# Turning the gate units of the second block with VectorE's block turn and ScalarE's copies

## The chip, the cores and the metric

The kernel runs on one core of a Trainium2 chip. The metric is the device time of one execution in microseconds. The kernel before takes 2195.05 us (median of 3 runs, 2194.01 to 2198.27).

## The reference, cut to what matters

Two blocks of a network run one after the other on 256 tokens of width 2048, everything in float32. The first is a gated linear attention with a convolution branch and a feed-forward part. The second, where the change is, makes eight projections of its input, runs two attentions (16 heads of a dilated one, 16 heads of a neighbourhood one), multiplies their outputs by silu of the two gate projections, multiplies that by `w_out` and ends in a layer norm:

```python
def second_block(x, w_in, w_out, t5_bias, na_rpb, ln_gain, ln_bias):
    ...
        h = jnp.einsum('bsd,de->bse', x, w_in[layer])
        qa, ka, va, ga, qb, kb, vb, gb = jnp.split(h, splits, axis=-1)
        ya = _dilated_attention(heads(qa, N_HEADS_A), heads(ka, N_HEADS_A), heads(va, N_HEADS_A), t5_bias)
        yb = _neighbourhood_attention(heads(qb, N_HEADS_B), heads(kb, N_HEADS_B), heads(vb, N_HEADS_B), na_rpb[layer])
        ya = merge(ya) * jax.nn.silu(ga.astype(jnp.float32))
        yb = merge(yb) * jax.nn.silu(gb.astype(jnp.float32))
        y = jnp.concatenate([ya, yb], axis=-1).astype(x.dtype)
        out = jnp.einsum('bse,ed->bsd', y, w_out[layer])
        x = _layer_norm(DEEPNORM_ALPHA * x + out, ln_gain[layer], ln_bias[layer])
```

## The kernel before, in words

**Units and steps.** All large products are cut into 96 units, the list `UNITS`: a unit is one 256 x 512 piece of a product, over 2048 rows of a weight. A unit has four steps, one for each 512 x 512 piece of the weight, so there are 384 steps, numbered s. Unit u has the steps 4u to 4u+3. The end of the list is: the units q2, k2, v2 of four head groups (steps 304 to 351), the gate units y0 to y3 (352 to 367), and the output units out0 to out3 (368 to 383).

**One step.** A float32 value is held as a sum of two numbers that TensorE multiplies fast (`hi` and `lo`). For each step SyncE loads 1 MB of weight into one of three `raw` buffers, ScalarE copies it to `whi` (`split`, L715), VectorE subtracts to get `wlo` (L981), and TensorE runs 24 matmuls (L1438 to L1440: 4 pieces of the contraction, 2 halves of the tokens, 3 products of hi and lo). In their program ScalarE and VectorE split for step s+2 while they are at step s; the split of step s+2 may begin when TensorE is through with step s-1, since the three buffers are used in turn. TensorE's `products(s)` waits for `s_lo`, which VectorE's split raises.

**Jobs.** The function `jobs(s)` lists what else each engine does at step s. Each engine walks through the steps in order and does its share of each job in the order in which its own function (`pool`, `scalar`, `vector`, `tensor`) is written. There is no scheduler: what stands first in the program of an engine runs first. The table `LATER` gives the jobs that follow a unit.

**The two ways to turn a unit.** The left operand of a product has to lie with the contraction on the partitions, so results have to be turned. The q, k and y units are turned by TensorE: `turn` (L1448) transposes eight 128 x 128 pieces into two of the four `side` banks of PSUM. The q2 and k2 units are turned in two parts: `block_turn` (L1203), one VectorE instruction that turns the 32 x 32 blocks in place into a buffer, and `carry` (L744), 16 ScalarE copies of 32 partitions x 256 elements that bring each block to its partitions, four in each of the jobs block, carry1, carry2, carry3.

**The gate units.** `post` of unit yj, at step 4u+3, applies silu on ScalarE (L793) and writes a `tmp` buffer. Two steps later the job `turn_y` follows, at steps 357, 361, 365 and 369 for y0 to y3: TensorE turns, VectorE multiplies YT (the attention's output, already turned) by the bank, in two halves (`times_gate`, L1169), ScalarE copies the product to `setA_hi` (L918), VectorE subtracts to `setA_lo` (L1360). In steps 357 and 361, which also have an attention job, `gate_turns(s)` puts the collection of the attention's values (`one_half`, L816 and L817, and `add_halves`, L1159) and `times_gate` ahead of the split. The output unit out0 needs in its step 368+c the product of gate unit yc, by the semaphore `s_yl` (`ready`, asked by TensorE in `products`).

**The attention.** Its last jobs are at steps 352 to 361: `att` 24 to 33. The values of the last pair of heads come at step 361.

Of the kernel before, what the change touches and what calls it, by code (L numbers as in the profile page):

```python
# [27 lines left out]
         "k2": ("block", "carry1", "carry2", "carry3"), "y": ("none", "turn_y")}  # L28
# [4 lines left out]
def jobs(s):  # L33
# [65 lines left out]
    for u in range(max(0, s // 4 - 2), s // 4 + 1):  # L99
        kind, j = UNITS[u]  # L100
        later = LATER.get(kind, ())
        if kind == "down" and j >= 12:
            later = ("flip", "flip_split")
        n = s - 4 * u - 4 if u > 0 else s - 7
        if 0 <= n < len(later):
            out.append((later[n], u))
# [4 lines left out]


def gate_turns(s):

    return any(job == "turn_y" for job, a in jobs(s))
# [74 lines left out]
def two_block_program(nc, T, C, out):  # L190
# [8 lines left out]
    with ctx:  # L199
# [24 lines left out]
        A_raw = at("setA_raw", "A", 16 * KB, [128, 16, 256])  # L224
        B_raw = at("setB_raw", "B", 16 * KB, [128, 16, 256])
# [141 lines left out]
        s_vh, s_yv, s_yh, s_yl = sem("s_vh"), sem("s_yv"), sem("s_yh"), sem("s_yl")  # L367
# [66 lines left out]
        def ready(u, kk):  # L434
# [17 lines left out]
            if kind == "out" and j == 0:  # L452
                return s_yl, part + 1
            return None

        def blocks(u):

            kind, j = UNITS[u]
            if kind in ("q2", "k2"):
                blk, turned = (qTb, qTr) if kind == "q2" else (kTb, kTr)  # L460
                return blk[j % 2][:, :, :, :, :], turned[j % 2][:, :, :], 1.0

# [242 lines left out]
        def scalar(e):  # L705
# [116 lines left out]
            for s in range(NS):  # L822
                for job, a in jobs(s):
                    if job == "att" and a % 2 and gate_turns(s):
                        one_half((a - 3) // 2)
# [7 lines left out]
                for job, a in jobs(s):  # L833
# [76 lines left out]
                    elif job == "turn_y":  # L910
                        j = UNITS[a][1]
                        e.wait_ge(*set_free(a))
                        e.wait_ge(s_xf, 2)
                        e.wait_ge(*full("values", 11 if j < 2 else 15))
                        for b in range(2):
                            k = 4 * j + 2 * b
                            e.wait_ge(*seen("turn", a, b))
                            e.activation(A_hi[:, k:k + 2, :], YT[:, k:k + 2, :], ACT.Copy).then_inc(s_yh, 1)  # L918
# [15 lines left out]
                    elif job == "att":  # L934
                        if a % 2 and a >= 3 and not gate_turns(s):
                            one_half((a - 3) // 2)
# [36 lines left out]
        def vector(e):  # L973
# [188 lines left out]
            def times_gate(u):  # L1162
                j = UNITS[u][1]
                e.wait_ge(*seen("values", 4 * j + 3))
                for b in range(2):
                    n = SN["turn", u, b]
                    v = YT[:, 4 * j + 2 * b:4 * j + 2 * b + 2, :]
                    e.wait_ge(*full("turn", u, b))
                    e.tensor_tensor(v, two(side[n % 4][:, :]), v, ALU.mult).then_inc(s_read[n % 4], 1)  # L1169

# [24 lines left out]
            def block_turn(u):  # L1195
# [5 lines left out]
                elif kind in ("q2", "k2"):  # L1201
                    e.wait_ge(s_xf, 2)
                e.transpose(blk.rearrange("p k t r n -> p t k (r n)"),  # L1203
# [25 lines left out]
            for s in range(NS):  # L1229
# [10 lines left out]
                for job, a in jobs(s):  # L1240
                    if job == "att" and a % 2 and gate_turns(s):
                        add_halves((a - 3) // 2)
                for job, a in jobs(s):
                    if job == "turn_y" and a < UI["y", 2]:
                        times_gate(a)
# [13 lines left out]
                for job, a in jobs(s):  # L1259
# [93 lines left out]
                    elif job == "turn_y":  # L1353
                        j = UNITS[a][1]
                        if j >= 2:
                            times_gate(a)
                        for b in range(2):
                            k = 4 * j + 2 * b
                            e.wait_ge(s_yh, 2 * j + b + 1)
                            e.tensor_tensor(A_lo[:, k:k + 2, :], YT[:, k:k + 2, :], asf(A_hi[:, k:k + 2, :]),  # L1360
# [292 lines left out]
```

## Time and profile before

| what | value |
|---|---|
| median of 3 runs | 2195.05 us |
| the execution that was profiled | 2196.3 us |
| its span, first to last instruction | 2193.6 us |
| granted TensorE clock, mean | 0.998 |
| TensorE busy | 2180.3 us, 99% of the span |
| VectorE busy | 1526.8 us, 70% |
| ScalarE busy | 1045.8 us, 48% |
| GpSimd busy | 228.4 us, 10% |
| chain that ended last | TensorE 91%, VectorE 5%, ScalarE 2% |

The profiled execution is 2.7 us longer than its span and 1.25 us above the median. A busy TensorE is not TensorE at its peak, because matmuls overlap: one of 128 x 512 is shown with 390 ns, but the next starts 227 ns after it.

### The profile page before, as it was taken

What the parts mean: (1) busy time and instruction counts of PE and PEld (TensorE: products, weight loads), DVE (VectorE), ACT (ScalarE), POOL (GpSimd) and SP (SyncE); (2) the same over time, 40 slices, a digit from 0 to 9 for tenths busy, and PEclk for the clock granted to TensorE, in tenths of its full rate; (3) what the DMA queues carried; (4) which work ended last, traced back from release to release, by engine and by line L of the source; (5) the groups of instructions that cost most, each with busy time, mean ns of one, the idle gap of its engine ahead of it and who ended that gap; (6) DMA issues with size and microseconds to landing.
All of it is one profiled execution on the core that took longest, in us unless ns stands there. A gap on an engine that the chain in (4) does not pass through costs nothing.

```text
span 2193.6 us, 24281 instructions
## 1 busy us (share of the span) xinstructions
PE 2180.3 (99%) x9962; PEld 1807.0 (82%) x9962; DVE 1526.8 (70%) x1613; ACT 1045.8 (48%) x1046; POOL 228.4 (10%) x253
## 2 busy tenths in 40 slices
PE   9999999999999999999999999999999999999998
PEld 8888888888888888888888888888888888888886
DVE  5577648646667747888855864864788778887755
ACT  7455554333333433444433433433444667767543
POOL 1023010000000000000100000000100122253201
PEclk9999999999999999999999999999999999999999
DMA  9555465777878776655555556566556756656663
GB/s 322 191 174 173 154 185 191 227 221 222 246 222 241 217 214 202 226 196 189 195 197 187 200 196 195 176 211 192 192 175 225 253 185 196 195 170 195 221 230 115
DMA packets 217102, 444.88 MB, mean 203 GB/s; under 512 B 9316, under 2 KB 10484, under 8 KB 216096
## 3 DMA queue, kind: packets, MB, share of 16 engines
q1 hardware_dynamic: 206976, 411.07, 56.6%
q0 software_dynamic: 9728, 32.18, 6.1%
q8 instruction: 78, 1.28, 0.2%
q14 instruction: 32, 0.26, 0.0%
q10 hardware_dynamic: 288, 0.10, 0.0%
HBM read 427.08 MB, written 12.06 MB: 200 GB/s over the span
## 4 chain that ended last, share of the span: by engine, by line
PE 91%; DVE 5%; ACT 2%; issue 1%; DMA 1%; POOL 0%; POOLq 0%; DVEq 0%; ACTq 0%
PE acc L1438 29%; PE acc L1439 29%; PE acc L1440 29%; DVE setB_raw L1192 1%; DVE wlo L981 1%; ACT whi L715 1%; PE side L1462 1%; DMA raw<-in_w_in 1%; PE side L1510 0%; PE side L1524 0%; PE side L1496 0%; DVE mx L1406 0%; ACT qTr L744 0%; DVE Sm L1402 0%; DVE PTl L1151 0%
## 5 line engine op out<-in xcount | busy, mean ns | idle before, releaser
L981 DVE TENSOR_TENSOR wlo<-raw,whi 128x2048 fp32r<-128x2048 f32 x380 | 892.9, 2352 | 512.0 <-ACT whi L715 510.7
L715 ACT ACTIVATE whi<-raw 128x2048 fp32r<-128x2048 f32 x380 | 726.8, 1914 | 668.6 <-PE acc L1440 641.2
L1438 PE MATMUL acc<-whi,setA_lo 128*128 128x512 f32 x1792 | 699.1, 390 | 0.1
L1440 PE MATMUL acc<-whi,setA_hi 128*128 128x512 f32 x1792 | 697.3, 389 | 0.0
L1439 PE MATMUL acc<-wlo,setA_hi 128*128 128x512 f32 x1792 | 697.3, 389 | 0.0
L1438 PE MATMUL acc<-whi,setB_lo 128*128 128x512 f32 x1280 | 501.2, 392 | 2.1 <-DVE wlo L981 1.1
L1439 PE MATMUL acc<-wlo,setB_hi 128*128 128x512 f32 x1280 | 498.6, 390 | 0.0
L1440 PE MATMUL acc<-whi,setB_hi 128*128 128x512 f32 x1280 | 498.1, 389 | 0.0
L1438 PEld LDWEIGHTS acc<-whi,setA_lo 128*128 128x128 f32 x1792 | 336.4, 188 | 71.2 <-DVE wlo L981 0.8
L1440 PEld LDWEIGHTS acc<-whi,setA_hi 128*128 128x128 f32 x1792 | 336.3, 188 | 70.3
L1439 PEld LDWEIGHTS acc<-wlo,setA_hi 128*128 128x128 f32 x1792 | 336.4, 188 | 68.7
L1438 PEld LDWEIGHTS acc<-whi,setB_lo 128*128 128x128 f32 x1280 | 240.3, 188 | 55.5 <-DVE setB_lo L1376 2.1
L1440 PEld LDWEIGHTS acc<-whi,setB_hi 128*128 128x128 f32 x1280 | 240.3, 188 | 50.5
L1439 PEld LDWEIGHTS acc<-wlo,setB_hi 128*128 128x128 f32 x1280 | 240.3, 188 | 48.6
L1192 DVE STREAM_TRANSPOSE setA_raw<-tmp 32x256 f32<-32x256 f32 x320 | 139.4, 436 | 9.4
L666 POOL TENSOR_TENSOR tmp<-tmp 128x1024 f32<-128x1024 f32 x16 | 30.4, 1897 | 733.4 <-DVE tmp L1109 733.4
L929 ACT ACTIVATE setA_hi<-setA_raw 128x1024 fp32r<-128x1024 f32 x20 | 21.3, 1063 | 96.2 <-DVE setA_raw L1192 96.2
L609 POOL TENSOR_TENSOR bia<-bia,msk 128x512 f32<-128x512 f32 x32 | 52.6, 1643 | 81.9 <-DMA bia<-t_scratch 44.9
L1192 DVE STREAM_TRANSPOSE setB_raw<-X 32x256 f32<-32x256 f32 x128 | 55.9, 436 | 3.8
L1192 DVE STREAM_TRANSPOSE setB_raw<-tmp 32x256 f32<-32x256 f32 x128 | 55.8, 436 | 3.8
L947 ACT ACTIVATE Sm<-Sm,nmx 128x256 f32<-128x256 f32 x64 | 32.1, 502 | 51.0 <-DVE nmx L1409 51.0
L646 POOL TENSOR_TENSOR DD<-cum 128x2048 f32<-128x2048 f32 x8 | 36.4, 4553 | 145.6 <-DVE cum L1293 91.2
(210 smaller groups left out, 1088.6 us busy)
## 6 DMA issues: line engine op xcount, KB each, us to landing
raw<-in_w_in SPq DMA_DIRECT2D x188, 1024.0 KB, 5.3
raw<-in_w_ffn_up SPq DMA_DIRECT2D x64, 1024.0 KB, 5.2
raw<-in_w_ffn_down SPq DMA_DIRECT2D x64, 1024.0 KB, 5.1
raw<-in_w_gla_out SPq DMA_DIRECT2D x16, 1024.0 KB, 5.1
raw<-in_w_conv_out SPq DMA_DIRECT2D x16, 1024.0 KB, 5.1
raw<-in_w_o SPq DMA_DIRECT2D x16, 1024.0 KB, 5.1
raw<-in_w_out SPq DMA_DIRECT2D x16, 1024.0 KB, 5.1
t_scratch<-t5v POOLq DMA_DIRECT2D x8, 512.0 KB, 7.2
```

The source lines that it names most:

```text
L609: e.tensor_tensor(bia[b][:, :, :], bia[b][:, :, :], msk[h // 16][:, :, :], ALU.add).then_inc(s_mb, 1)
L646: e.tensor_tensor(dv, cv, ref, ALU.subtract).then_inc(s_xd, 1)
L666: e.tensor_tensor(tm, tm, tm, ALU.mult).then_inc(s_pq, 1)
L715: e.activation(whi[r][:, :, :], raw[r][:, :, :], ACT.Copy).then_inc(s_hi, 1)
L929: e.activation(hi[:, k:k + 4, :], turned[:, k:k + 4, :], ACT.Copy).then_inc(s_fh, 1)
L947: e.activation(Sm[b][:, t, :], Sm[b][:, t, :], ACT.Exp, bias=nmx[b][:, t:t + 1], accum_out=den[b][:, t:t + 1]).then_inc(s_ex, 1)
L981: e.tensor_tensor(wlo[r][:, :, :], raw[r][:, :, :], asf(whi[r][:, :, :]), ALU.subtract).then_inc(s_lo, 1)
L1192: e.transpose(dst[32 * r:32 * r + 32, :, :, q, :], src[32 * q:32 * q + 32, :, :, r, :]).then_inc(s_fl, 1)
L1438: e.matmul(o, xl, whi[r][:, k, :], start=kk == 0, stop=False)
L1439: e.matmul(o, xh, wlo[r][:, k, :], start=False, stop=False)
L1440: f = e.matmul(o, xh, whi[r][:, k, :], start=False, stop=kk == 15)
L1462: f = e.matmul(bank[:, 128 * h:128 * h + 128], row[:, 0:128], row[:, 128:256], start=dd == 0, stop=dd == 1)
```

## The change

The gate units now take the second way of turning. TensorE's turns of the y units (32 transposes, four groups of eight) are gone, and with them their use of the `side` banks. For each gate unit there are three jobs instead: `block01` (VectorE's block turn of the unit's `tmp` into `A_blk`, then eight of ScalarE's carrying copies into `A_raw`), in the next step `carry23` (the other eight copies), and in the step behind that `gate_y` (VectorE multiplies YT by `A_raw`, ScalarE copies the whole 128 x 1024 to `setA_hi`, VectorE subtracts to `setA_lo`). The buffers lie in region A, which the attention uses until its end, and the jobs stand at steps 362, 363, 364 for y0, 364, 365, 366 for y1, 366, 367, 368 for y2 and 368, 369, 370 for y3. `gate_y` stands ahead of the split in the programs of both engines. `gate_turns` is gone, so the attention jobs of steps 357 and 361 stand behind the split as in all other steps. A new semaphore `s_yg` joins the multiplication to the copy.

```diff
-         "k2": ("block", "carry1", "carry2", "carry3"), "y": ("none", "turn_y")}
+         "k2": ("block", "carry1", "carry2", "carry3"), "y": ()}
...
-    for u in range(max(0, s // 4 - 2), s // 4 + 1):
+    for u in range(max(0, s // 4 - 3), s // 4 + 1):
...
+        if kind == "y":
+            later = ("none",) * (6, 4, 2, 0)[j] + ("block01", "carry23", "gate_y")
...
-def gate_turns(s):
-
-    return any(job == "turn_y" for job, a in jobs(s))
...
+        A_blk = at("setA_blk", "A", 0, [128, 16, 2, 4, 32])
...
-                return s_yl, part + 1
+                return s_yl, kk // 4 + 1
...
+            if kind == "y":
+                return A_blk[:, 4 * j:4 * j + 4, :, :, :], A_raw[:, 4 * j:4 * j + 4, :], 1.0
...
                 for job, a in jobs(s):
-                    if job == "att" and a % 2 and gate_turns(s):
-                        one_half((a - 3) // 2)
+                    if job == "gate_y":
+                        k = 4 * UNITS[a][1]
+                        e.wait_ge(s_yg, UNITS[a][1] + 1)
+                        e.activation(A_hi[:, k:k + 4, :], YT[:, k:k + 4, :], ACT.Copy).then_inc(s_yh, 1)
                 if s < 2:
                     fine(s + 2)
...
-                    elif job == "turn_y":
-                        j = UNITS[a][1]
-                        e.wait_ge(*set_free(a))
-                        e.wait_ge(s_xf, 2)
-                        e.wait_ge(*full("values", 11 if j < 2 else 15))
-                        for b in range(2):
-                            k = 4 * j + 2 * b
-                            e.wait_ge(*seen("turn", a, b))
-                            e.activation(A_hi[:, k:k + 2, :], YT[:, k:k + 2, :], ACT.Copy).then_inc(s_yh, 1)
...
-            def times_gate(u):
...
+                if kind == "y":
+                    e.wait_ge(*set_free(u))
+                    e.wait_ge(s_xf, 2)
+                    e.wait_ge(*full("values", 11 if j < 2 else 15))
                 e.transpose(blk.rearrange("p k t r n -> p t k (r n)"),
                             tmp_of(u)[:, :, :].rearrange("p t (k n) -> p t k n", k=4)).then_inc(s_bt, 1)
...
                 for job, a in jobs(s):
-                    if job == "att" and a % 2 and gate_turns(s):
-                        add_halves((a - 3) // 2)
-                for job, a in jobs(s):
-                    if job == "turn_y" and a < UI["y", 2]:
-                        times_gate(a)
+                    if job == "gate_y":
+                        j = UNITS[a][1]
+                        v = YT[:, 4 * j:4 * j + 4, :]
+                        e.wait_ge(*seen("values", 4 * j + 3))
+                        e.wait_ge(s_bm, 16 * BN[a] + 16)
+                        e.tensor_tensor(v, A_raw[:, 4 * j:4 * j + 4, :], v, ALU.mult).then_inc(s_yg, 1)
+                        e.wait_ge(s_yh, j + 1)
+                        e.tensor_tensor(A_lo[:, 4 * j:4 * j + 4, :], v, asf(A_hi[:, 4 * j:4 * j + 4, :]),
+                                        ALU.subtract).then_inc(s_yl, 1)
```

ScalarE's row before, from the split of step 368 to that of step 372 (L715 is a split, L793 silu of y3, L918 the copy of a gated product):

```order
L715 ACTIVATE whi_54<-raw_51 128x2048
L715 ACTIVATE whi_52<-raw_49 128x2048
L793 ACTIVATE tmp_65<-acc,rstd_150 128x512 x2
L715 ACTIVATE whi_53<-raw_50 128x2048
L715 ACTIVATE whi_54<-raw_51 128x2048
L918 ACTIVATE setA_hi<-YT 128x512 x2
L715 ACTIVATE whi_52<-raw_49 128x2048
```

The same stretch of ScalarE now (L744 are eight carrying copies, of y2 in the first two rows of it and of y3 in the last two; L827 is the copy of the gated product, of y2 and then of y3):

```order
L715 ACTIVATE whi_54<-raw_51 128x2048
L744 ACTIVATE setA_raw<-setA_blk 32x2x4x32 x8
L715 ACTIVATE whi_52<-raw_49 128x2048
L744 ACTIVATE setA_raw<-setA_blk 32x2x4x32 x8
L793 ACTIVATE tmp_66<-acc,rstd_151 128x512 x2
L827 ACTIVATE setA_hi<-YT 128x1024
L715 ACTIVATE whi_53<-raw_50 128x2048
L744 ACTIVATE setA_raw<-setA_blk 32x2x4x32 x8
L715 ACTIVATE whi_54<-raw_51 128x2048
L744 ACTIVATE setA_raw<-setA_blk 32x2x4x32 x8
L827 ACTIVATE setA_hi<-YT 128x1024
L715 ACTIVATE whi_52<-raw_49 128x2048
```

Between the same five splits stand 32 carrying copies that were not there, and one gated product's copy more.

VectorE's row before, from the split of step 368 to that of step 372 (L981 is a split, L1169 the two multiplications by the turned gate y3, L1360 its two subtractions):

```order
L981 TENSOR_TENSOR wlo_57<-raw_51,whi_54 128x2048
L981 TENSOR_TENSOR wlo_55<-raw_49,whi_52 128x2048
L981 TENSOR_TENSOR wlo_56<-raw_50,whi_53 128x2048
L981 TENSOR_TENSOR wlo_57<-raw_51,whi_54 128x2048
L1169 TENSOR_TENSOR YT<-side,YT 128x512 x2
L1360 TENSOR_TENSOR setA_lo<-YT,setA_hi 128x512 x2
L981 TENSOR_TENSOR wlo_55<-raw_49,whi_52 128x2048
```

The same stretch of VectorE now (L974 is the split, L1191 the block turn of y3, L1234 the multiplication and L1236 the subtraction, of y2 and then of y3):

```order
L974 TENSOR_TENSOR wlo_57<-raw_51,whi_54 128x2048
L974 TENSOR_TENSOR wlo_55<-raw_49,whi_52 128x2048
L1191 STREAM_TRANSPOSE setA_blk<-tmp_66 128x2x4x128
L1234 TENSOR_TENSOR YT<-setA_raw,YT 128x1024
L1236 TENSOR_TENSOR setA_lo<-YT,setA_hi 128x1024
L974 TENSOR_TENSOR wlo_56<-raw_50,whi_53 128x2048
L974 TENSOR_TENSOR wlo_57<-raw_51,whi_54 128x2048
L1234 TENSOR_TENSOR YT<-setA_raw,YT 128x1024
L1236 TENSOR_TENSOR setA_lo<-YT,setA_hi 128x1024
L974 TENSOR_TENSOR wlo_55<-raw_49,whi_52 128x2048
```

The block turn of y3 and the gate of y2 stand ahead of the split of step 370, and the gate of y3 stands behind the split of step 371, ahead of that of step 372.

## Rows read from the trace of the kernel before

**Rows 1.** The page's first part: busy time of each engine.
```profile
PE 2180.3 (99%) x9962; PEld 1807.0 (82%) x9962; DVE 1526.8 (70%) x1613; ACT 1045.8 (48%) x1046; POOL 228.4 (10%) x253
```

**Rows 2.** All waits of TensorE: us in total, times, longest.
```profile
PE acc L1453 <- DVE tmp L975: 1.5, 1, 1.5
PE acc L1438 <- DVE wlo L981: 1.1, 1, 1.1
PE acc L1438 <- DVE setB_lo L1376: 0.8, 3, 0.4
```

**Rows 3.** Timeline of TensorE, turns of y1 and y3: start us, us, line.
```profile
2061.40 1.04 PE L1448 MATMUL side<-ident,tmp 128*128 128x128 f32 x8
2062.19 0.48 PE L1438 MATMUL acc<-whi,setB_lo 128*128 128x512 f32 x1
...
2106.75 1.03 PE L1448 MATMUL side<-ident,tmp 128*128 128x128 f32 x8
2107.54 0.48 PE L1438 MATMUL acc<-whi,setA_lo 128*128 128x512 f32 x1
...
2113.08 0.39 PE L1438 MATMUL acc<-whi,setA_lo 128*128 128x512 f32 x1
...
2118.52 0.39 PE L1438 MATMUL acc<-whi,setA_lo 128*128 128x512 f32 x1
```

**Rows 4.** Groups by line and shape: count, busy us, mean ns, idle before.
```profile
L981 DVE TENSOR_TENSOR wlo<-raw,whi 128x2048 fp32r<-128x2048 f32 x29 | 67.0, 2314 | 42.8 <-ACT whi L715 42.8
L1203 DVE STREAM_TRANSPOSE qTb<-tmp 128x1024 f32<-128x1024 f32 x4 | 5.0, 1246 | 0.1
L1257 DVE TENSOR_TENSOR qTl<-qTr,qTa 128x1024 fp32r<-128x1024 f32 x4 | 4.9, 1226 | 1.4 <-ACT qTa L749 1.4
L744 ACT ACTIVATE qTr<-qTb 32x256 f32<-32x256 f32 x64 | 26.6, 416 | 9.8 <-DVE qTb L1203 8.3
L749 ACT ACTIVATE qTa<-qTr 128x1024 fp32r<-128x1024 f32 x4 | 4.2, 1062 | 0.1
```

**Rows 5.** Timeline of ScalarE, carrying copies of k2 among splits.
```profile
1978.65 1.74 ACT L744 ACTIVATE kTr<-kTb 32x256 f32<-32x256 f32 x4 [0.80 <-DVE kTb L1203]
1980.42 1.92 ACT L715 ACTIVATE whi<-raw 128x2048 fp32r<-128x2048 f32 x1
1982.36 1.75 ACT L744 ACTIVATE kTr<-kTb 32x256 f32<-32x256 f32 x4
1984.13 1.92 ACT L715 ACTIVATE whi<-raw 128x2048 fp32r<-128x2048 f32 x1
```

**Rows 6.** Timeline of ScalarE, end of the attention and the gate units.
```profile
2062.01 0.38 ACT L817 ACTIVATE YT<-side 64x256 f32<-64x256 f32 x1
...
2068.03 1.93 ACT L715 ACTIVATE whi<-raw 128x2048 fp32r<-128x2048 f32 x1 [0.85 <-PE acc L1440]
2073.41 1.27 ACT L793 ACTIVATE tmp<-acc,rstd 128x512 f32<-128x512 f32 x2 [3.45 <-PE acc L1440]
...
2118.80 1.92 ACT L715 ACTIVATE whi<-raw 128x2048 fp32r<-128x2048 f32 x1 [3.54 <-PE acc L1440]
```

**Rows 7.** Timeline of VectorE, the same stretch.
```profile
2062.41 0.86 DVE L1159 TENSOR_TENSOR YT<-side,YT 64x256 f32<-64x256 f32 x2 [2.79 <-ACT YT L817]
```

**Rows 8.** Timeline of TensorE, its last matmul.
```profile
2183.57 0.39 PE L1440 MATMUL acc<-whi,setA_hi 128*128 128x512 f32 x1
```

**Rows 9.** Weight loads, first line and a turn's: ns min/median/max, first and last start.
```profile
L1453 PEld LDWEIGHTS acc<-tmp x22: 192/333/333, 1.5 to 5.7; 128*128 128x128 f32 x22
...
L1448 PEld LDWEIGHTS side<-ident,tmp x32: 138/140/142, 2033.7 to 2107.4; 128*128 128x128 f32 x32
```

**Rows 10.** Stretches at the end: PE, PEld, DVE, ACT, POOL busy; PEclk, DMA, GB/s.
```profile
2180.00:2186.50 6.50, 3.96 (x18) 2.95 (x16) 4.52 (x11) 0.20 (x1) 2.75 (x4) 1.00 0.44 161
2186.50:2187.50 1.00, 0.00 (x0) 0.00 (x0) 0.96 (x3) 0.95 (x2) 0.22 (x1) 0.57 0.00 0
2187.50:2193.00 5.50, 0.00 (x0) 0.00 (x0) 3.01 (x5) 0.25 (x1) 3.19 (x4) 0.50 0.53 191
```

More of the change, by code:

```diff
@@ L366, in two_block_program @@
         s_pn, s_ph, s_pl = sem("s_pn"), sem("s_ph"), sem("s_pl")
-        s_vh, s_yv, s_yh, s_yl = sem("s_vh"), sem("s_yv"), sem("s_yh"), sem("s_yl")
+        s_vh, s_yv, s_yg, s_yh, s_yl = (sem(n) for n in ("s_vh", "s_yv", "s_yg", "s_yh", "s_yl"))
         s_var, s_sd, s_rs, s_nmu = sem("s_var"), sem("s_sd"), sem("s_rs"), sem("s_nmu")
@@ L934, in scalar @@
                     elif job == "att":
-                        if a % 2 and a >= 3 and not gate_turns(s):
+                        if a % 2 and a >= 3:
                             one_half((a - 3) // 2)
@@ L1160, in add_halves @@
                 c.then_inc(s_read[n % 4], 1)
-            def times_gate(u):
[L1163 to L1169, printed above, removed]
             def flip(u, half):
@@ L1352, in vector @@
                             e.tensor_tensor(z[:, :, :], z[:, :, :], z1[:, :, :], ALU.add).then_inc(s_cu, 1)
[L1353 to L1360, printed above, removed]
-                                            ALU.subtract).then_inc(s_yl, 1)
                     elif job == "flip":
@@ L1387, in vector @@
                     elif job == "att":
-                        if a % 2 and a >= 3 and not gate_turns(s):
+                        if a % 2 and a >= 3:
                             add_halves((a - 3) // 2)
```

## The prediction

> **What bounds the kernel now.** I read the busy shares first: TensorE 2180.3 us, 99% of the span, ScalarE at 48% and VectorE at 70% [rows 1]. Then the waits of TensorE: 3.4 us in the whole execution, the longest 1.5 [rows 2]; around the turn of y3 its steps follow each other without a gap [rows 3]. So TensorE's own instructions are the bound, and two things count: what is taken off TensorE, and whether another engine now makes it wait. An average of 48% on ScalarE does not answer the second; that is a question for the eight or nine steps in which the new work stands. The reader is to see in the timelines that in those steps ScalarE waits 3.5 us per step for TensorE [rows 6], which is the cover that the new work has to fit in.
>
> **What is removed from TensorE.** A turn of eight transposes starts at 2106.75 and the next product at 2107.54: 0.79 us. The step after a turn takes 5.54 us (2107.54 to 2113.08), an ordinary one 5.44 (2113.08 to 2118.52): 0.10 more [rows 3]. So 0.89 a turn, and 3.6 us for four. All of it is on the bound: minus 3.6 us.
>
> **What is added to the others.** For each gate unit ScalarE gets 16 carrying copies. Four stand 1.77 us apart from what follows (1978.65 to the split at 1980.42, 1982.36 to 1984.13), so 0.44 us each, 3.54 for eight and 7.1 for sixteen [rows 5]. The two half copies to setA_hi become one of 1.06 us [rows 4]. VectorE gets a block turn of 1.25, and its four half instructions become two of 1.23 [rows 4]. A split takes ScalarE 1.94 us until a carrying copy follows (1980.42 to 1982.36) [rows 5], and VectorE 2.29 (the group's mean is 2.31) [rows 4].
>
> From step 364 on a gate unit falls every two steps. In these ScalarE has 2 x 1.93 of splits, 7.1 of copies, 1.06 for the gate and, for y2 and y3, 1.27 for silu [rows 6]: about 12.0 us, or 13.3 with silu, and TensorE needs 10.9 for two steps. ScalarE is overbooked there, and what it is late by adds up, since no step in between gives time back.
>
> The lead that it starts with: it may split for step s+2 from the end of step s-1 plus 0.4 (2068.03 is 0.4 after the start of step 363, which is 2062.19 plus 5.44) [rows 3, 6]. ScalarE and VectorE then need 4.2 us of the 10.9 that there are until the step is due: a lead of some 6 us.
>
> I walk through it with TensorE's start of step 362 as zero. On the trace before this is 2061.40, where the turn of y1 stood [rows 3], and in time another 0.9 us earlier because the turn of y0 is gone too. The attention's last values leave ScalarE at 1.0 (2062.39) and VectorE at 1.9 (2063.27) [rows 6, 7]. Step 362+n is due at 5.44 n.
>
> - y0: ScalarE splits 364 until 2.9, copies until 6.7, splits 365 until 8.6, copies until 12.2, silu of y2 until 13.4. VectorE's multiplication, waiting for the copies, is done at 13.4; the gate's copy runs until 14.4.
> - y1: split 366 until 16.3, copies 19.8, split 367 until 21.75, copies 25.3. VectorE does the block turn of y2 while that runs, multiplies until 26.55; the gate's copy until 27.6.
> - y2: split 368 until 29.4, copies 32.95, split 369 until 34.9, copies 38.4, silu of y3 until 39.7. Now VectorE has to turn y3 (it stands ahead of the gate in its program) and multiply: 42.1. ScalarE has waited 2.4 us for it, copies the gate until 43.15, and splits 370 until 45.0. VectorE's part ends at 47.3. Step 370 is due at 43.55. **TensorE stands for 3.8 us.**
> - y3: copies until 48.5, split 371 until 50.45, copies until 54.0, multiplication 55.25, gate's copy 56.3, VectorE's subtraction 57.6. Step 371 needs the product of y3 at its start, since its part of the contraction is just that unit. It is due at 47.35 plus 5.44, 52.8. **TensorE stands for 4.8 us.**
>
> After that ScalarE has only splits. That of step 372 is through both engines at 60.4 and due at 63.1, that of 373 at 62.6: nothing is late behind it. Together 8.6 us. Behind the two waiting instructions of VectorE (the multiplications of y2 and y3) stand the splits of 370 and of 372; the first is what TensorE waits for, the second has 2.7 us left.
>
> A rule of the Trainium skill speaks against this sum. The page "ScalarE: Activation LUTs", section "What ACT_TABLE_LOAD costs", says that an activation with immediate operands takes 186 ns plus 0.833 per element, and that such instructions overlap back to back by about 93 ns. That would be an estimated 0.31 us a carrying copy, not 0.44, and with it the same walk leaves one stop of 2.1 us, a gain of 1.5 us in all. The trace does not agree: 1.74 us for four of 0.416 leaves 0.44 from start to start, so no overlap [rows 4, 5].
>
> **What a stop costs besides.** The first matmul after a stop needs its weights first: between 0 and 0.19 us more, the first product's 0.48 against 0.39 being the nearest row [rows 3]; 0.1 each, 0.2 in all. The clock: the trace shows no stop of this length between matmuls. The nearest rows are the ends of the kernel. After TensorE's last matmul (over at 2183.96) the granted clock is 1.00 until 2186.5, 0.57 in the next microsecond and 0.50 after, the lower level of 1.2 GHz [rows 8, 10]; so it fell about 3 us after work ended, and both stops are longer. At the start the weight loads take 333 ns against 140 for a turn's, and this lasts from 1.5 to 5.7 [rows 9]; I read it as work at the lower level for 4.2 us, which loses 2.1. A fall in the first stop costs nothing: the end of the second one is set by ScalarE's row (57.6) and not by TensorE, so a slower step 370 only makes the second stop shorter. A fall in the second costs between 0 and 2.1; I take 1.0, the middle, as I can't tell how the shorter step before it counts.
>
> A rule of the page "TensorE: Matmul & The Clock Gate", section "Part 1: The HAM clock gate (the "warmup" mystery)", says that an idle TensorE is brought to half of its clock and comes back after sustained work. The end of the trace agrees with the first half, 0.50 [rows 10].
>
> **Where I cost at nothing.** The attention jobs of steps 357 and 361 now stand behind the split, as in the other steps; TensorE waits nowhere there [rows 2], and the split of 363, which began only after the halves at 2062.39, comes earlier. SyncE's loads follow VectorE's splits: the latest, for 373, is asked for at 47.3, 10.8 us ahead of its use at 58.1. If that cover were gone, step 373 would be late by what the load exceeds it. GpSimd has no new work.
>
> **Sum.** -3.6 + 8.6 + 0.2 + 1.0 = +6.2 us. Against the profiled execution: its span goes from 2193.6 to 2199.8 and its time from 2196.3 to 2202.5. It lies 1.25 above the median of the runs, so the median goes from 2195.05 to 2201.2.
>
> **The rivals.**
> - *ScalarE keeps up* (the other side). One mechanism: the carrying copies of a gate unit cost less than those of q2 and k2. Every 0.01 us on one copy moves the stops by about 0.5 us (16 copies in each of three to four units that are late). Zero net is at 0.34 us a copy; at 0.31 the stop is 2.1 and the time is 2195.05 - 3.6 + 2.1 + 0.1 = 2193.7; with no stop at all 2191.4. For it: the operands lie in another region, and ScalarE is less disturbed after the attention. Against it: the 64 copies of q2 take 416 ns in the mean by the same line, and the shape is the same [rows 4].
> - *The stops are shorter than I walk them and have no price in clock*: VectorE and ScalarE hand over faster at three or four places, 0.3 us each, and the clock stays: 8.6 - 1.2 - 3.6 + 0.2 = +4.0, 2199.1. For it: each hand-over in the walk is taken as a full wait.
> - *The clock falls for longer*: two full ramps count, or the lower clock also meets the steps before the stops, +2.1 twice in place of 1.0: 2195.05 - 3.6 + 8.6 + 0.2 + 4.2 = 2204.4. For it: the end of the kernel shows the fall. Against it: the first fall is hidden by the second stop.
>
> **How the numbers follow.** Forecast 60%, shorter stops 17%, longer clock 12%, ScalarE keeps up 11%. What a measurement of this kernel can tell from no change is 0.2%, 4.4 us. Slower by more, over 2199.4: nearly all of the forecast, the longer clock and a third of the shorter stops: 0.75. Within: the rest of these and nearly all of "keeps up": 0.23. Faster by more than 4.4 us would need more than the turns cost altogether: 0.02. The range goes from 2196.0, which leaves out most of "keeps up", to 2204.5, the longer clock.
>
> **What the profile would show.** Right: no L1448 in the gate units; TensorE waits for VectorE's split at step 370, some 3.8 us, and for setA_lo at 371, some 4.8 (or a sum near 8.6, less what a slower step 370 takes up); ScalarE busy without a gap from step 362 but for the waits on the multiplications; step 372 on unchanged. Wrong: carrying copies at 0.31 us from start to start; a wait of TensorE before step 369 or after 371; no wait at all, which would mean that the lead is larger than 6 us.

## The result, and the profile after

The changed kernel takes 2201.28 us (median of 13 executions, 2199.92 to 2202.43), the kernel before 2195.38 us beside it (13 executions, 2194.01 to 2198.27): a ratio of 1.0026 [1.0019, 1.0033]. It is slower by 5.9 us. The forecast was 2201.2.

Part of a time lies outside the span from the first to the last instruction. In all 13 executions of the changed kernel this part is 1.8 us; in the 21 executions of the kernel before beside the first experiments it is between 1.8 and 3.2. By spans the loss is therefore a little larger than by times: 2199.5 us in the median now, against 2193.1 to 2193.4 for the kernel before beside the experiments. Why the kernel before has the longer part in some executions stays open.

The page of the kernel after begins with the span and the busy shares (against [rows 1]):

```profile
span 2199.3 us, 24267 instructions
...
PE 2180.4 (99%) x9930; PEld 1807.7 (82%) x9930; DVE 1528.5 (70%) x1609; ACT 1071.4 (49%) x1106; POOL 226.4 (10%) x253
```

TensorE has 32 instructions fewer, ScalarE 60 more. The busy shares hardly move, so the cause can't be read from them. The waits of TensorE in the kernel after (us in total, times, longest), against [rows 2]:

```profile
PE acc L1421 <- DVE wlo L974: 3.9, 2, 3.7
PE acc L1421 <- DVE setA_lo L1236: 3.0, 1, 3.0
PE acc L1436 <- DVE tmp L968: 1.5, 1, 1.5
PE acc L1421 <- DVE setB_lo L1359: 0.8, 3, 0.4
```

The last two were there before. New are one wait of 3.7 us for a split's low part, and one of 3.0 us for the gated product's low part. TensorE's timeline around them (start us, us, line; in brackets the idle time and its releaser; L1421 to L1423 are the matmuls of a step):

```profile
2059.68 0.40 PE L1421 MATMUL acc<-whi,setB_lo 128*128 128x512 f32 x1
...
2103.01 0.39 PE L1423 MATMUL acc<-whi,setA_hi 128*128 128x512 f32 x1
2107.05 0.77 PE L1421 MATMUL acc<-whi,setA_lo 128*128 128x512 f32 x1 [3.65 <-DVE wlo L974]
2107.61 0.63 PE L1422 MATMUL acc<-wlo,setA_hi 128*128 128x512 f32 x1
...
2110.09 0.40 PE L1422 MATMUL acc<-wlo,setA_hi 128*128 128x512 f32 x1
...
2113.77 0.39 PE L1423 MATMUL acc<-whi,setA_hi 128*128 128x512 f32 x1
2117.12 0.80 PE L1421 MATMUL acc<-whi,setA_lo 128*128 128x512 f32 x1 [2.96 <-DVE setA_lo L1236]
```

The first row is the start of step 362, the zero of the prediction's walk. The next two are the last matmul of step 369 and the first of step 370: a matmul would have started 0.22 or 0.23 us after 2103.01, at 2103.23, and it started at 2107.05, a stop of 3.82 from start to start. The second stop is 2117.12 less 2113.99, 3.13. After both stops a matmul takes 0.63 in place of 0.39, and the next starts 0.43 after it in place of 0.23. Step 370 lasts 6.94 (2107.05 to 2113.99) and step 371 lasts 7.03 (to the start of step 372 at 2124.15), an ordinary one 5.44.

What ScalarE does in that stretch of the kernel after (L715 is a split, L744 the carrying copies, L793 silu, L827 the gate's copy):

```profile
2062.87 3.49 ACT L744 ACTIVATE setA_raw<-setA_blk 32x256 f32<-32x256 f32 x8 [0.26 <-DVE setA_blk L1191]
...
2097.97 1.26 ACT L793 ACTIVATE tmp<-acc,rstd 128x512 f32<-128x512 f32 x2
2101.72 1.06 ACT L827 ACTIVATE setA_hi<-YT 128x1024 fp32r<-128x1024 f32 x1 [2.48 <-DVE YT L1234]
2102.68 1.90 ACT L715 ACTIVATE whi<-raw 128x2048 fp32r<-128x2048 f32 x1
2104.48 3.47 ACT L744 ACTIVATE setA_raw<-setA_blk 32x256 f32<-32x256 f32 x8
2107.97 1.91 ACT L715 ACTIVATE whi<-raw 128x2048 fp32r<-128x2048 f32 x1
2109.91 3.48 ACT L744 ACTIVATE setA_raw<-setA_blk 32x256 f32<-32x256 f32 x8
2114.75 1.06 ACT L827 ACTIVATE setA_hi<-YT 128x1024 fp32r<-128x1024 f32 x1 [1.36 <-DVE YT L1234]
```

Where ScalarE waited for TensorE before [rows 6], its idle time is now almost only that in front of the gate's copies, where it waits for VectorE's multiplication. The split of step 370 begins at 2102.68, half a microsecond before TensorE wants both of its parts. And VectorE in the kernel after:

```profile
2099.33 1.25 DVE L1191 STREAM_TRANSPOSE setA_blk<-tmp 128x1024 f32<-128x1024 f32 x1 [2.56 <-ACT tmp L793]
2100.50 1.18 DVE L1234 TENSOR_TENSOR YT<-setA_raw,YT 128x1024 f32<-128x1024 f32 x1
2102.81 1.23 DVE L1236 TENSOR_TENSOR setA_lo<-YT,setA_hi 128x1024 fp32r<-128x1024 f32 x1 [1.13 <-ACT setA_hi L827]
2104.61 2.29 DVE L974 TENSOR_TENSOR wlo<-raw,whi 128x2048 fp32r<-128x2048 f32 x1 [0.57 <-ACT whi L715]
...
2115.84 1.23 DVE L1236 TENSOR_TENSOR setA_lo<-YT,setA_hi 128x1024 fp32r<-128x1024 f32 x1 [1.12 <-ACT setA_hi L827]
```

Step 370's last part is ready at 2106.90 and TensorE starts at 2107.05; step 371's at 2117.07, start 2117.12. The two engines are a chain here, each waiting for the other (2.48, 1.13, 0.57), and it is the chain that sets TensorE.

The clock, in stretches of the kernel after (us, then PE, PEld, DVE, ACT, POOL busy, granted clock, DMA share, GB/s):

```profile
2106.50:2107.00 0.50, 0.00 (x0) 0.00 (x0) 0.40 (x1) 0.48 (x2) 0.00 (x0) 0.58 0.00 0
...
2108.00:2112.00 4.00, 4.00 (x15) 3.20 (x14) 2.08 (x1) 3.88 (x6) 0.00 (x0) 0.75 0.80 259
2112.00:2116.00 4.00, 2.15 (x10) 1.45 (x8) 1.60 (x3) 2.57 (x6) 0.00 (x0) 1.00 0.63 204
2116.00:2120.00 4.00, 2.88 (x7) 2.31 (x8) 3.42 (x3) 3.41 (x2) 0.00 (x0) 0.60 0.15 58
2120.00:2124.00 4.00, 4.00 (x19) 3.25 (x18) 2.13 (x1) 0.00 (x0) 0.00 (x0) 0.97 0.72 229
```

The granted clock is still 1.00 in the half microsecond before the first of these rows. So it falls while TensorE still stands, before the restart at 2107.05, and it is back within the step that follows; the same happens at the second stop (0.82 from 2116.50 to 2117.00).

**The ledger.** The span grew from 2193.6 to 2199.3, by 5.7. The start of step 362 lies at 2059.68; before, with y0's turn taken off, it would be at 2060.51 [rows 3], so this execution was 0.83 ahead for another reason (the kernel before shows a wait of 1.1 us for a split [rows 2], before step 346, that this one lacks). Then: four turns, minus 3.6; stops 3.82 and 3.13; two slow steps of 1.50 and 1.59 more. -0.8 - 3.6 + 3.8 + 3.1 + 3.1 = +5.6. Taken over the changed stretch alone, from the start of step 357 to that of step 373, the trace before has 96.67 us and this one 103.13: +6.5, which the four turns, the two stops and the two slow steps account for in full.

### The profile page after: what moved, and what is told of

Read it like the earlier page. It is cut to its first block, busy times and chain, and to the rows that moved or that the text cites. A ratio compares the mean times of both kernels' runs of the same rounds, so it can differ in the third digit from the quotient of the medians.

```text
span 2199.3 us, 24267 instructions
## 1 busy us (share of the span) xinstructions
PE 2180.4 (99%) x9930; PEld 1807.7 (82%) x9930; DVE 1528.5 (70%) x1609; ACT 1071.4 (49%) x1106; POOL 226.4 (10%) x253
## 4 chain that ended last, share of the span: by engine, by line
PE 92%; DVE 3%; DMA 2%; ACT 1%; issue 1%; SPq 0%; POOL 0%; POOLq 0%; DVEq 0%; ACTq 0%
PE acc L1421 30%; PE acc L1423 30%; PE acc L1422 30%; DMA raw<-in_w_in 2%; DVE setB_raw L1176 1%; DVE wlo L974 1%; ACT whi L715 1%; PE side L1507 1%; PE side L1445 1%; PE side L1479 1%; PE side L1493 1%; ACT setA_raw L744 0%; DVE setB_lo L1359 0%; PE side L1431 0%; SPq L533 0%
## 5 line engine op out<-in xcount | busy, mean ns | idle before, releaser
L974 DVE TENSOR_TENSOR wlo<-raw,whi 128x2048 fp32r<-128x2048 f32 x380 | 891.1, 2347 | 511.3 <-ACT whi L715 509.7
L715 ACT ACTIVATE whi<-raw 128x2048 fp32r<-128x2048 f32 x380 | 726.7, 1914 | 660.8 <-PE acc L1423 633.6
L1421 PE MATMUL acc<-whi,setA_lo 128*128 128x512 f32 x1792 | 701.3, 391 | 6.8 <-DVE wlo L974 3.9
L1423 PE MATMUL acc<-whi,setA_hi 128*128 128x512 f32 x1792 | 698.9, 390 | 0.0
L1421 PE MATMUL acc<-whi,setB_lo 128*128 128x512 f32 x1280 | 501.3, 392 | 0.8 <-DVE setB_lo L1359 0.8
L1423 PE MATMUL acc<-whi,setB_hi 128*128 128x512 f32 x1280 | 498.5, 389 | 0.0
L1421 PEld LDWEIGHTS acc<-whi,setA_lo 128*128 128x128 f32 x1792 | 337.6, 188 | 77.8 <-issue 4.0
L1423 PEld LDWEIGHTS acc<-whi,setA_hi 128*128 128x128 f32 x1792 | 337.3, 188 | 70.3
L1421 PEld LDWEIGHTS acc<-whi,setB_lo 128*128 128x128 f32 x1280 | 240.4, 188 | 53.7 <-DVE setB_lo L1359 2.1
L1423 PEld LDWEIGHTS acc<-whi,setB_hi 128*128 128x128 f32 x1280 | 240.4, 188 | 50.4
```

Source lines behind the costliest of these rows:

```text
L715: e.activation(whi[r][:, :, :], raw[r][:, :, :], ACT.Copy).then_inc(s_hi, 1)
L974: e.tensor_tensor(wlo[r][:, :, :], raw[r][:, :, :], asf(whi[r][:, :, :]), ALU.subtract).then_inc(s_lo, 1)
L1421: e.matmul(o, xl, whi[r][:, k, :], start=kk == 0, stop=False)
L1423: f = e.matmul(o, xh, whi[r][:, k, :], start=False, stop=kk == 15)
```

## The experiments

All ran beside the kernel before, which took 2195.2 to 2195.65 us in the median.

### Earlier and evenly: `spread`

```diff
-            later = ("none",) * (6, 4, 2, 0)[j] + ("block01", "carry23", "gate_y")
+            later = (("none",) * (1, 1, 0)[j] + ("block", "carry1", "carry2", "carry3", "gate_y")) if j < 3 \
+                else ("block01", "carry23", "gate_y")
```

> The same work in the same amount, only earlier and thinner: y0, y1 and y2 carry four copies a step (steps 357 to 360, 361 to 364, 364 to 367), their gates at 361, 365 and 368; y3 as in the change (368, 369, 370). Theory (ScalarE's row is overbooked in steps 362 to 370, and that alone makes the two stops): ScalarE now has 1.93 + 1.77 us of a 5.44 us step, both stops vanish or stay under 1 us together, the clock stays at 1.00, and only the 3.6 us of the turns are left: 2191.8 us, against 2195.4 of the kernel before. Rival (the block turn and the long way of a gated unit through two engines is what is late, whatever the load): the stop at step 371 stays at 3 us or more, 2197 to 2199.

Measured: 2200.65 us (2198.14 to 2202.64), ratio 1.0024 [1.0015, 1.0033]. A miss by 9 us. The profiled execution is the fastest of the eleven, so what the median holds beyond it is not seen. Its waits of TensorE, and ScalarE's row at the gate of y2:

```profile
PE acc L1422 <- DVE setA_lo L1237: 2.9, 1, 2.9
PE acc L1422 <- DVE wlo L975: 2.7, 2, 1.7
PE side L1508 <- DVE PTl L1145: 1.6, 1, 1.6
```

```profile
2055.45 1.73 ACT L745 ACTIVATE setA_raw<-setA_blk 32x256 f32<-32x256 f32 x4
2057.21 1.09 ACT L936 ACTIVATE PT<-side 128x512 fp32r<-128x512 f32 x2
...
2100.20 1.06 ACT L828 ACTIVATE setA_hi<-YT 128x1024 fp32r<-128x1024 f32 x1 [2.48 <-DVE YT L1235]
```

Two mistakes of mine. The steps to 361 have no room as I took it: four carrying copies stand there ahead of the attention's copies to PT, and TensorE waits for these. And the gate of y2, at step 368, stands on VectorE behind the block turn of y3, which waits for that step's silu; so ScalarE still stands 2.48 us before the split of step 370. The same order costs more at step 361, where ScalarE stands 5.39 us ahead of the gate of y0 and the next split; the waits for `wlo` are those of the steps 362 and 363. y2's copies were early and y2's gate was not. What this run does show: the stop for wlo at step 370 went with ScalarE's lateness; that at 371 stayed.

### The split first: `gate_behind`

`gate_y` moved behind the split on ScalarE and VectorE, the jobs in the same steps:

```diff
+                if s < 2:
+                    fine(s + 2)
+                elif s + 2 < NS:
+                    split(s + 2)
                 for job, a in jobs(s):
...
```

> The change with one part undone: the gate (multiplication, copy, subtraction) stands behind the split of its step on ScalarE and VectorE, as the turned gate did for y2 and y3 before. Theory: the copy of y3 now waits behind the split of step 372, which may start only when TensorE is through with step 369, and each gate comes one split later; walked through, five stops of 0.3, 4.5, 3.2 and 8.5 us in steps 367 to 371, some 21 us with the clock, so 2195.4 - 3.6 + 20 = 2212 us (2208 to 2215). Rival (the order does not matter, ScalarE has the same sum of work): 2201.3 as the change.

Measured: 2212.96 us (2212.22 to 2213.59), ratio 1.008 [1.0066, 1.0094]. A hit. The expectation speaks of five stops and gives four sizes; the trace has four: some 0.25 us ahead of step 367, and 4.15, 2.62 and 7.97 ahead of the steps 369, 370 and 371. The waits:

```profile
PE acc L1422 <- DVE setA_lo L1243: 10.6, 2, 8.0
PE acc L1422 <- DVE wlo L974: 4.2, 1, 4.2
```

So the place of the gate ahead of the splits is not what costs; without it the change would cost three times as much. Of the two engines' work, the gated product is what TensorE needs first.

### Half the copies: `half_copies`

Eight copies of 64 partitions in place of sixteen of 32 for a gate unit. Half of the blocks don't reach their own place, so the output is not that of the reference; all the rest of the work is done.

```diff
-                    for r in range(4):
+                    for r in (range(2) if UNITS[u][0] == "y" else ()):
+                        e.activation(to[64 * r:64 * r + 64, :, :, q, :],
+                                     fr[64 * (q // 2):64 * (q // 2) + 64, :, :, 2 * r, :], ACT.Copy,
+                                     scale=scale).then_inc(s_bm, 1)
...
```

> The change with 8 carrying copies for a gate unit in place of 16, each of 64 partitions x 256 (half of the blocks are not brought to their place). VectorE's part and the order are untouched. Theory: a copy takes the same 0.42 us on 64 partitions, ScalarE's row is 3.5 us shorter a unit, the stops shrink from 6.9 us to under 0.5 and the clock stays up: 2191.8 to 2192.3 us. Rival (VectorE's row, or the hand-overs, bound the gate): at least half of the stops stays, 2197 or more.

Measured: 2191.82 us (2189.88 to 2194.25), ratio 0.9984 [0.9975, 0.9993]. A hit, and the best evidence for the cause: everything moved by the change is still where it was, only ScalarE's 8 copies a unit are gone, and the time is 9.5 us lower. From step 357 to step 373 its trace has 93.25 us, 3.4 less than the kernel before and 9.9 less than the changed one. TensorE's waits are all small, and the copies of 64 partitions take as long as those of 32:

```profile
...
PE acc L1425 <- DVE wlo L978: 0.7, 2, 0.5
```

```profile
2099.84 1.73 ACT L744 ACTIVATE setA_raw<-setA_blk 64x256 f32<-64x256 f32 x4
2101.59 1.92 ACT L715 ACTIVATE whi<-raw 128x2048 fp32r<-128x2048 f32 x1
```

### A dose between: `copies12`

Twelve copies a gate unit (eight for half of the blocks, four wide ones for the others, whose blocks partly don't reach their place).

```diff
+                    wide = UNITS[u][0] == "y" and q < 2
+                    for r in (range(2) if wide else ()):
+                        e.activation(to[64 * r:64 * r + 64, :, :, q, :], fr[0:64, :, :, 2 * r, :], ACT.Copy,
+                                     scale=scale).then_inc(s_bm, 1)
+                    for r in (() if wide else range(4)):
...
```

> Dose: the change with 12 carrying copies a gate unit in place of 16 (4 of 64 partitions in the first job, 8 of 32 in the second; half of the blocks of the first job are not brought to their place). With 8 the stops were gone. Theory: walked through, the lead at step 370 is just kept (0.3 us) and one stop of 2.8 us is left at 371; whether the clock falls in it is open (0 or 1.5 us): 2195.4 - 3.6 + 2.8 = 2194.6, or 2196.1. Rival (a threshold and not a sum: either all stops or none): 2191.8 or 2201.3.

Measured: 2195.6 us (2193.69 to 2197.7), ratio 1.0001 [0.9992, 1.001]. So 8, 12 and 16 copies take 2191.8, 2195.6 and 2201.3. The profiled execution (2197.25 us) has one long stop, and the clock falls in it:

```profile
2113.37 0.80 PE L1425 MATMUL acc<-whi,setA_lo 128*128 128x512 f32 x1 [2.62 <-DVE setA_lo L1240]
```

```profile
2112.00:2116.00 4.00, 2.63 (x6) 2.17 (x7) 3.33 (x2) 3.66 (x3) 0.00 (x0) 0.61 0.23 89
```

The executions lie 4 us apart, and the two expected values, with a fall of the clock and without, both lie within; which executions had it can't be told, since only one was profiled. That execution also has 2.1 us of waits for splits ahead of step 352, where nothing was changed, so its own time says little on the dose.

### Keeping TensorE at work in the stops: `filler` and `filler13`

28, and in the second kernel 13, float32 matmuls of the identity ahead of steps 370 and 371, into a bank that nobody reads.

```diff
+                if s in (370, 371):
+                    if s == 370:
+                        e.wait_ge(s_read[0], max(n for n in SN.values() if n % 4 == 0) // 4 + 1)
+                    for i in range(28):
+                        e.matmul(side[0][:, 0:128], ident[:, :], ident[:, :], start=True, stop=True)
```

> The change with 28 matmuls of 128 x 128 (identity by identity, into a bank of PSUM that nothing reads) on TensorE ahead of step 370 and again ahead of step 371, some 3.1 us each, so that it works through most of each stop. Theory: the stops themselves are set by ScalarE's row (TensorE starts step 371 at the same moment), so the filler costs nothing; the granted clock stays at 1.00, step 371 takes 5.44 us and not 6.94: 1.5 us faster than the change, 2199.8. The lower clock in step 370 was free, so no more than that. Rival A (both lower clocks cost): 2198.3. Rival B (the clock falls all the same, or costs nothing): 2201.3.

Measured: 2204.14 us (2203.32 to 2204.34), ratio 1.0039 [1.0027, 1.0052]. A miss: I had sized the filler too small. It took longer than the stops and became the bound itself:

```profile
2103.90 6.42 PE L1519 MATMUL side<-ident 128*128 128x128 f32 x56
```

56 records for 28 matmuls, 0.22 us each, 6.17 in all. Two of these less the turns, 12.3 - 3.6 = 8.7, is nearly what the span grew by (8.9, 2202.5 against 2193.6). Hence the run with 13:

> As the filler before, with 13 float32 matmuls and not 28: the trace showed that one takes 0.22 us (two records), so that the 28 took 6.2 us, longer than the stop that they were to fill. 13 take 2.9 us. Theory: TensorE starts step 371 at the moment that ScalarE's row sets, as in the change; the filler costs nothing, the clock stays at 1.00, step 371 takes 5.44 us and not 6.94: 1.5 us faster than the change, 2199.8. Rival (the lower clock of step 370 costs too): 2198.3. Rival (the clock costs nothing): 2201.3.

Measured: 2200.35 us (2198.97 to 2201.49), ratio 1.0021 [1.0012, 1.003]. Stops and fillers in its profile:

```profile
2103.43 3.07 PE L1519 MATMUL side<-ident 128*128 128x128 f32 x26
2107.33 0.47 PE L1421 MATMUL acc<-whi,setA_lo 128*128 128x512 f32 x1 [0.84 <-DVE wlo L974]
...
2112.90 3.07 PE L1519 MATMUL side<-ident 128*128 128x128 f32 x26
2117.45 0.50 PE L1421 MATMUL acc<-whi,setA_lo 128*128 128x512 f32 x1 [1.48 <-DVE setA_lo L1236]
```

Work of 3 us put into each stop costs nothing: step 371 starts 57.58 after the zero (2059.87 here), against 57.44 in the changed kernel. The steps 370 and 371 last 5.57 and 5.56, 0.12 more than an ordinary one, which is the restart, and the clock stays at 1.00. The gain is what the lower clock cost in step 371: 7.03 less 5.56, 1.5 us, by the two profiles, and 0.9 us by the medians. The ranges of the executions overlap and the two kernels ran at different times, so the sign and the size are borne out only roughly.

### Two of the turns back on TensorE: `turns_kept`

The old turns of y2 and y3, eight transposes each, put back at steps 365 and 369 with nobody reading them; the rest as in the changed kernel.

```diff
+                if s in (365, 369):
+                    u = UI["y", 2 if s == 365 else 3]
+                    e.wait_ge(*evacuated(u))
...
+                            e.transpose(side[b][:, 128 * i:128 * i + 128],
...
```

> The change, with TensorE's eight transposes of y2 (after step 365) and of y3 (after step 369) put back, into a bank that nothing reads. Theory: the start of step 371 is set by ScalarE's row and not by TensorE, so 1.8 us of TensorE's work ahead of it is free: 2201.3, no change. Rival (the saving on TensorE and the stops add up): 2203.1.

Measured: 2201.86 us (2200.09 to 2203.9), ratio 1.003 [1.0019, 1.0042]. TensorE's own work grows by 1.8 us and the median by 0.6. In its profile the stop ahead of step 370 became 1.99, and step 371 starts at 2116.97, zero plus 57.58 once more (zero is 2059.39 here). So at these steps the end is not TensorE's; taking turns off it there gives nothing back by the start of step 371. What differs comes behind it: the second stop is 4.38 and the lower clock lasts longer, so step 371 takes 8.27 in place of 7.03.

### Nothing late, by my own table: `placed`

Each unit's jobs put where I saw room, y0 from step 356, y3 as it was.

```diff
+            later = (("block", "carry1", "carry2", "carry3", "none", "none", "gate_y"),
+                     ("none", "block01", "carry23", "gate_y"),
+                     ("block01", "carry23", "gate_y"), ("block01", "carry23", "gate_y"))[j]
```

> The same work as in the change, placed where the trace of the first spread version shows room: y0 carries four copies a step at 356 to 359 and none at 360, where four copies had stood ahead of the last probabilities of the attention and TensorE waited 1.6 us for them; its gate is at 362; y1 is turned at 361 and 362, gate at 363; y2 at 364 and 365, gate at 366, so that it is through before silu of y3; y3 at 368, 369, gate 370. Theory (only where ScalarE's row is full does TensorE stop): walked through, the closest places are the splits of 365 and 368 and the product of y3 at step 371, each 0.1 to 0.3 us before it is due; stops of 0 to 1 us in all, clock 1.00, so 2191.8 to 2192.8 us against 2195.3. Rival (y3's own way, from silu at 368 to the subtraction, is longer than the three steps it has, whatever stands before): a stop of some 3 us at 371 remains as in the first spread version, 2195 us.

Measured: 2199.22 us (2197.29 to 2201.46), ratio 1.0016 [1.0007, 1.0025]. The second miss of the same kind as `spread`:

```profile
PE acc L1423 <- DVE wlo L976: 7.6, 7, 2.0
```

```profile
2053.17 1.74 ACT L746 ACTIVATE setA_raw<-setA_blk 32x256 f32<-32x256 f32 x4
...
2060.00 1.08 ACT L937 ACTIVATE PT<-side 128x512 fp32r<-128x512 f32 x2
```

Even two groups of copies, at steps 358 and 359, push the last copies to PT so far back that the splits behind them come late until step 368. Of the seven waits four, 4.9 us together, are in the steps 362 to 368; the other three, 2.8 us, come before step 351, where this run moved nothing, and are not its doing. So four short waits have taken the place of two long ones. None of them is for the product of y3. That refutes a rival I had kept, that y3's way (turn, 16 copies, gate between the steps 368 and 371) is too long by itself; started in time it fits.

### Shared between the engines: `shared`

ScalarE carries y0 and y2 and most of y3. The whole of y1 and four blocks of y3 are turned by VectorE alone, each block straight to its partitions. Nothing of the new work is on ScalarE before step 361.

```diff
+Y_JOBS = {361: (("block01", 0), ("flips01", 1)), 362: (("carry23", 0), ("flips2", 1)), 363: (("gate_y", 0),),
+          364: (("block", 2), ("flips3", 1)), 365: (("carry12", 2),), 366: (("carry3", 2), ("gate_y", 1)),
+          367: (("gate_y", 2),), 368: (("block01", 3), ("flips3", 3)), 369: (("carry2", 3),), 370: (("gate_y", 3),)}
...
+                    for r in range(4):
+                        e.transpose(dst[32 * r:32 * r + 32, :, :, q, :],
+                                    src[32 * q:32 * q + 32, :, :, r, :]).then_inc(s_fl, 1)
```

> A version that takes what the placed one taught: nothing in steps 356 to 360, where ScalarE's row feeds the attention's last probabilities and VectorE's split of 362 waits behind them, and the load shared. y0: block turn at 361, eight copies at 361 (ahead of the last halves, where ScalarE idles 5 us) and eight at 362, gate 363. y1: no copies of ScalarE, 16 of VectorE's partition-crossing transposes (0.44 us each) at 361, 362 and 364, gate 366. y2: block turn 364, copies 4, 8, 4 at 364 to 366, gate 367, ahead of silu of y3. y3: block turn 368, 12 copies at 368 and 369, four transposes of VectorE at 368, gate 370. Theory (the stops come from ScalarE's full row, so with 20 copies fewer and each step under 5.44 us they go): the smallest lead, walked through, is 1.4 us at step 371, no stop, only the turns' 3.6 us are left: 2191.8 us against 2195.4, faster than both kernels. Rival (y3's own way is too long for its three steps, or the neighbourhood of the attention's end cannot take anything): a stop of 1 to 3 us, 2193 to 2195.

Measured: 2192.61 us (2191.41 to 2193.35), ratio 0.9985 [0.9976, 0.9994]. A hit, and faster than both kernels; against the kernel before it gains 3.0 us in times and 2.4 in the spans' medians. Two of its waits, and what a block costs on VectorE:

```profile
PE acc L1445 <- DVE wlo L978: 0.7, 1, 0.7
PE side L1503 <- DVE YT L1156: 0.5, 1, 0.5
```

```profile
2100.42 1.85 DVE L1196 STREAM_TRANSPOSE setA_raw<-tmp 32x256 f32<-32x256 f32 x4
```

A block is 0.46 us on VectorE against 0.44 on ScalarE; it isn't cheaper there, it only stands on the engine with room. The second wait comes at step 358, ahead of all the new work, and belongs to the attention job of step 357 that the change moved behind the split; `filler`, whose program is that of the changed kernel up to there, has it too:

```profile
PE side L1479 <- DVE YT L1152: 0.6, 1, 0.6
```

## Why the prediction was right, point by point

- **The bound.** Right: TensorE sets the end but where an overbooked ScalarE makes it wait. `half_copies` shows that it is the number of ScalarE's copies: with eight fewer a unit, and all else of the change in place, the loss of 5.9 us becomes a gain of 3.4.
- **The turns, -3.6.** Borne out by `half_copies`, where nothing else of size is left: 2195.2 - 2191.8 = 3.4 by times, 3.1 by the spans' medians, 3.4 in the traces from step 357 to 373.
- **The carrying copies at 0.44.** Right, eight in 3.49. The rule of the Trainium skill on overlapping activations ("ScalarE: Activation LUTs", section "What ACT_TABLE_LOAD costs") doesn't hold for this form here: eight in 3.49 leave 0.44 from start to start, where the page would give an estimated 0.31. The rival that was built on a lower price fell with it.
- **The walk.** In the trace, each less the zero of 2059.68:

| point | predicted | measured |
|---|---|---|
| ScalarE has split 364 | 2.9 | 2.93 |
| first eight copies of y0 | 6.7 | 6.68 |
| gate's copy of y2 done | 43.15 | 43.10 |
| step 370's last part ready | 47.3 | 47.22 |
| subtraction of y3 done | 57.6 | 57.39 |
| start of step 371 | 57.6 | 57.44 |

- **The first stop, 3.8.** Measured 3.82.
- **The second, 4.8.** Measured 3.13, and this is no miss of the walk: step 370 took 1.5 us longer at the lower clock, which the prediction said would only shorten the second stop. By start of step 371 the two agree within 0.2. `filler13` shows the converse: clock kept, step 371 at the same place.
- **Restart, +0.2 and clock, +1.0.** Together 1.2. In the profile step 371 was 1.6 longer: 0.1 for its restart (the restart of step 370, like its clock, is hidden by the second stop) and 1.5 for the clock; in the medians `filler13` gave back 0.9. The middle that I took was a guess between two ends, and that it came near is luck. The upper end, 2.1, rested on reading the slow start of the kernel as the lower clock; the granted clock is 1.00 there in the profile before (1.50 to 5.00), so that reading is not shown; and `turns_kept` has a fall that costs 2.8. The prediction also took both stops to be longer than the 3 us after which the clock had fallen at the kernel's end. The second was 2.96, and in `copies12` the clock fell in a stop of 2.62.
- **What was costed at nothing.** SyncE's loads: TensorE does not wait for them. Right. The attention jobs behind the split: nothing in the changed kernel's profile, but in those of `filler`, `placed` and `shared` TensorE waits 0.6, 0.7 and 0.5 us at step 358 for the addition of the attention's halves that the change moved behind the split. So this term is small, but not nothing in every execution.
- **The rivals.** "ScalarE keeps up" is refuted by the row of copies; "shorter stops" by the walk; "longer clock" failed because, as the walk has it, only the last slow step is paid.

That median and forecast differ by 0.1 is in part luck. Over the changed stretch the sum was 6.2 against a measured 6.5: the stops with the slow step 370 were 8.45 and not 8.6, restart and clock 1.6 and not 1.2. The forecast then carried over the 2.7 us outside the span of the one profiled execution, where the changed kernel has 1.8, and it started from a median of three runs, 2195.05, where thirteen give 2195.38. These have cancelled. What is not luck is the place and the kind of both stops, and the start of step 371.

## What to carry to other kernels

Before work is moved to an engine that is busy for half of the time, walk through the steps where it lands, one instruction after the other, with the lead that the buffers give; a mean share says nothing on it. Moving the same work to earlier steps is no cure unless what stands behind it there is priced as well: two of my tables failed by four copies ahead of the attention's. If two stops follow each other and another engine's chain sets the end of the second, whatever happens between them on the waiting engine (filler, slower clock, kept work) does not move the end of the second, as long as it fits: the filler of 6.2 us did not. Only its effect on the second stop's length, and so on the clock behind it, may be paid.

## What the runs showed of the hardware

- **The clock falls at stops within a kernel, and not by their length alone.** In single profiled executions the granted clock was at 0.5 (the level of 1.2 GHz) behind stops of 3.65 and 2.96 us (the kernel after), 2.62 (`copies12`), 4.38 (`turns_kept`) and 4.15, 2.62 and 7.97 (`gate_behind`), and 1.00 behind 1.99 (`turns_kept`), 1.48 (`filler13`), 1.79 and 1.98 (`placed`), and 2.88 (`spread`), whose restart and next stretch are these:

```profile
2115.63 0.50 PE L1422 MATMUL acc<-whi,setA_lo 128*128 128x512 f32 x1 [2.88 <-DVE setA_lo L1237]
```

```profile
2116.00:2120.00 4.00, 4.00 (x19) 3.31 (x18) 3.85 (x2) 1.93 (x2) 0.00 (x0) 1.00 0.12 10
```

  And these are the stop of 2.62 in `gate_behind` and a stretch behind it, where the clock, at 1.00 until the restart, fell only then:

```profile
2111.90 0.50 PE L1422 MATMUL acc<-whi,setA_lo 128*128 128x512 f32 x1 [2.62 <-DVE setA_lo L1243]
2112.50:2114.00 1.50, 1.50 (x5) 1.16 (x4) 0.00 (x0) 1.40 (x5) 0.00 (x0) 0.50 0.28 107
```

  What decides between 2.62 and 2.88 stays open. The scatter of the executions doesn't help: `spread` and `copies12` scatter by 4.5 and 4.0 us, but so do kernels without such a stop, the kernel before by 4.3 and `half_copies` by 4.4. What a fall costs differs too: about seven matmuls at 0.43 from start to start in place of 0.23 behind the stops of 2.62, 2.96 and 3.65, 1.5 us; about thirteen behind that of 4.38, where the 15th matmul of the step starts 5.96 us after the first in place of 3.2, 2.8 us. That is more than the 2.1 that the prediction took as the upper end, and the stop of 7.97 costs as much (step 371 of `gate_behind` takes 8.21). It also is one way in which `turns_kept` may lose its 0.6 us.
- **A copy of 64 partitions took as long as one of 32.** 32 x 256 and 64 x 256 both take 0.43 to 0.44 us from start to start; of these two only the count matters. Other heights were not run.
- **A float32 matmul of 128 x 128 by 128 x 128** is two records and takes 0.22 us, about as long as one of 128 x 512 in the split form.
